# Differential attention scores: both components of a step issued together, in the order full, full, half, half, behind the first projections

## What is computed

```python
def diff_attention(q, k, v, pos, rel_bias, lam):
    scale = DIFF_HEAD_DIM ** -0.5
    def block(args):                        # 128 queries
        qb, qp = args
        s = jnp.einsum('bqhcd,bkhcd->bhcqk', qb, k).astype(jnp.float32) * scale
        bias = jnp.transpose(rel_bias[bucket], (0, 3, 1, 2)).astype(jnp.float32)
        s = s + bias[:, :, None]
        s = jnp.where(causal[:, None, None], s, NEG_INF)
        p = jax.nn.softmax(s, axis=-1)
        a = (p[:, :, 0] - lam * p[:, :, 1]).astype(v.dtype)
        return jnp.einsum('bhqk,bkhe->bqhe', a, v)
```

## Time and profile before

| | us |
|---|---|
| median of three runs | 2902.03 |
| the three runs | 2899.20 to 2904.88 |
| the profiled execution | 2900.93 |
| its span in the trace | 2899.5 |
| differential attention stage in it | about 397 to 655 |

### The profile page before, as it was taken

How to read it: one execution, slowest core, us unless ns; L and a number is a source line. 1 busy time by engine, 2 the same in 40 slices (tenths; PEclk the granted TensorE clock), 3 DMA queues, 4 the chain that set the end, 5 groups by cost and what they waited for, 6 DMA issues and landing times.

```text
span 2899.5 us, 46216 instructions
## 1 busy us (share of the span) xinstructions
PE 2749.4 (95%) x16516; PEld 2246.6 (77%) x16517; DVE 1502.7 (52%) x2607; ACT 1055.9 (36%) x1670; POOL 297.3 (10%) x318
## 2 busy tenths in 40 slices
PE   7899989988999997999999999999999999999995
PEld 3366655555666454989999999999899999999994
DVE  5555535664111145666666666665454445544454
ACT  2144324443110120545555555553333333333333
POOL 1000000000000123011111111111011111111111
PEclk9999989989999995999999999999999999999997
DMA  4000010002111434666666666667999999999995
GB/s 138 1 10 5 15 30 15 1 1 66 44 43 43 174 57 144 226 203 203 216 218 203 203 207 210 206 215 226 312 335 345 339 342 342 338 342 342 342 343 174
DMA packets 423534, 523.14 MB, mean 180 GB/s; under 512 B 27716, under 2 KB 334408, under 8 KB 423432
## 3 DMA queue, kind: packets, MB, share of 16 engines
q1 hardware_dynamic: 403544, 464.31, 49.4%
q0 software_dynamic: 18880, 57.91, 8.3%
q10 hardware_dynamic: 1040, 0.00, 0.0%
HBM read 482.23 MB, written 39.95 MB: 180 GB/s over the span
## 4 chain that ended last, share of the span: by engine, by line
PE 58%; issue 0%; DMA 0%; DVE 0%; ACT 0%; SPq 0%; POOLq 0%; POOL 0%; ACTq 0%
PE banks L2001 21%; PE banks L2011 19%; PE banks L2052 17%; PE banks L1993 1%; DMA arena<-acc_rows 0%; DVE arena L2295 0%; DMA acc_rows<-arena,rows 0%; ACT parts L2096 0%; SPq L1933 0%; DVE parts L2216 0%; ACT arena L2188 0%; ACT parts L2123 0%; ACT arena L2167 0%; POOLq L1959 0%; DVE stat L2293 0%
## 5 line engine op out<-in xcount | busy, mean ns | idle before, releaser
L2001 PEld LDWEIGHTS banks<-arena 128*128 128x128 f32 x5376 | 604.9, 192 | 8.3 <-issue 6.7
L2001 PE MATMUL banks<-arena 128*128 128x128 f32 x5376 | 605.2, 275 | 6.3 <-issue 6.3
L2011 PE MATMUL banks<-parts 128*128 128x256 f32 x4608 | 558.6, 284 | 7.1 <-issue 4.0
L2011 PEld LDWEIGHTS banks<-parts 128*128 128x128 f32 x4608 | 557.9, 193 | 8.7 <-issue 4.4
L2052 PE MATMUL banks<-parts 128*128 128x512 f32 x2160 | 498.3, 391 | 0.0
L2052 PEld LDWEIGHTS banks<-parts 128*128 128x128 f32 x2160 | 403.0, 188 | 82.1
L2212 DVE TENSOR_TENSOR parts<-arena,parts 128x1024 fp32r<-128x1024 f32 x264 | 315.2, 1222 | 128.4 <-ACT parts L2116 128.4
L2235 DVE TENSOR_SCALAR arena<-banks,arena 128x128 f32<-128x128 f32 (+1 forms) x528 | 181.3, 392 | 335.6 <-PE banks L2001 335.6
L2216 DVE TENSOR_TENSOR parts<-arena,parts 128x1024 fp32r<-128x1024 f32 x192 | 233.7, 1222 | 197.6 <-ACT parts L2123 196.6
L2116 ACT ACTIVATE parts<-arena 128x1024 fp32r<-128x1024 f32 x264 | 269.7, 1054 | 88.4 <-PE banks L2052 44.9
L2123 ACT ACTIVATE parts<-arena 128x1024 fp32r<-128x1024 f32 x192 | 201.1, 1054 | 178.3 <-PE banks L2011 123.4
(11 more groups left out here) (306 smaller groups left out, 2763.8 us busy)
## 6 DMA issues: line engine op xcount, KB each, us to landing
arena<-in_w SPq DMA_DIRECT2D x264, 1024.0 KB, 7.6
arena<-in_w SPq DMA_DIRECT2D x66, 2048.0 KB, 12.8
arena<-in_w_in SPq DMA_DIRECT2D x27, 512.0 KB, 5.4
arena<-in_x SPq DMA_DIRECT2D x16, 512.0 KB, 6.8
h_rows<-arena POOLq DMA_DIRECT2D x10, 512.0 KB, 7.6
acc_rows<-arena SPq DMA_DIRECT2D x8, 512.0 KB, 6.0
arena<-acc_rows SPq DMA_DIRECT2D x8, 512.0 KB, 7.4
out<-arena SPq DMA_DIRECT2D x8, 512.0 KB, 6.0
```

What stands on the lines that cost most here:

```text
L2001: last = nc.tensor.matmul(bank(g, 2 * (c % 2) + s)[:, a * JOB:a * JOB + P], w1[c][:, s, k, a * P:(a + 1) * P], xt[:, k, 0:P], start=(k == ...
L2011: last = nc.tensor.matmul(bank(g, 2 * (c % 2) + s)[:, a * JOB:(a + 1) * JOB], first_part[p][:, y, k, :], x[:, k, :], start=(k == 0 and y = ...
```

## The change

Both components of a step are now issued by one call, behind the first projections of the step. In every stretch of up to 512 keys the two full passes stand first, then the two half passes. The call waits for both exponentials of the step before, and for the projected units that component 1 needs. VectorE's and ScalarE's lists are the same as before.

```diff
-                def score(u, c):
+                def score(u):
                     h, i = divmod(u, TT)
-                    keys, s = (end(i) + 1) * P, 2 * u + c
-                    pe.wait_ge(lo_made, units_before(u, c, general))
-                    if s >= 2:
-                        pe.wait_ge(exped, s - 1)
-                    rows, cols = (first, second)[c], slice(i * P, (i + 1) * P)
+                    keys, cols = (end(i) + 1) * P, slice(i * P, (i + 1) * P)
+                    pe.wait_ge(lo_made, units_before(u, 1, general))
+                    if u >= 1:
+                        pe.wait_ge(exped, 2 * u)
                     for a in range(0, keys, HALF):
                         n = min(HALF, keys - a)
-                        out = bank(g, 2 * c + a // HALF)[:, 0:n]
-                        nc.tensor.matmul(out, q_c[c][:, cols], k_c[h % 2][c][:, a:a + n], start=True, stop=False)
-                        last = nc.tensor.matmul(out, q_c[c][rows, cols], k_low[h % 2][rows, a:a + n], start=False, stop=True)
-                    last.then_inc(scored, 1)
+                        outs = [bank(g, 2 * c + a // HALF)[:, 0:n] for c in range(2)]
+                        for c in range(2):
+                            nc.tensor.matmul(outs[c], q_c[c][:, cols], k_c[h % 2][c][:, a:a + n], start=True, stop=False)
+                        for c, rows in ((0, first), (1, second)):
+                            last = nc.tensor.matmul(outs[c], q_c[c][rows, cols], k_low[h % 2][rows, a:a + n], start=False, stop=True)
+                            if a + n == keys:
+                                last.then_inc(scored, 1)
...
-                score(0, 0)
-                score(0, 1)
+                score(0)
                 for u in range(DIFF_STEPS):
-                    if u + 1 < DIFF_STEPS:
-                        score(u + 1, 0)
                     for n, k in fill[u][0]:
                         project(n, k)
                     if u + 1 < DIFF_STEPS:
-                        score(u + 1, 1)
+                        score(u + 1)
                     for n, k in fill[u][1]:
                         project(n, k)
```

## The result

The changed kernel is **slower**: 2920.9 us (four runs, 2920.5 to 2923.3) against 2903.5 for the kernel before, a ratio of 1.0064 with a 95% interval of 1.0047 to 1.0082. That is +17.5 us in the medians, where +9 was forecast. The side was right, the size was half. The profiled execution has a span of 2919.9 us against 2899.5.

A forecast was written before the change was run, and what follows sets the result against it. The prediction took TensorE to limit the stage on the average. Order +3, clock +6 and last head's clock +2 gave +11, less 1 or 2 for slow stretches on waiting work: +9, 2911 us, range 2894 to 2922.

The forecast's parts named there:

- The saving: TensorE's score groups: two row-count changes in place of four, saving 6.5 or 4.6 us per head, 26 or 18 in all.
- the lower bound of the pair: Score half passes on disjoint rows run at the same time, so the second starts 0.02 us behind the first.
- the stream price of 0.22: Upper bound for score half passes: the second starts 0.22 us behind the first, as passes in a stream do.
- The waits: TensorE idles behind the chain of additions, maxima and exponentials: 6.6 us more per middle head, 6.3 with slower half passes.
- Before score i=6: a wait of **1.8: Middle head, ahead of tile 6's score: TensorE has 3.1 us of work against a chain of 4.7 + 0.15.
- The first head's -2: First head's change from the new order alone: -2 or -0.5 us, from a 0.79 wait gone and waits added.
- The +3 for the order as a whole: All heads, new order without clock effects: -0.4 or +6.2 us by half-pass overlap, with +3 taken between.
- the clock: TensorE falls to its lower clock behind half of some nine new idles, 1.4 us each: +6, and +2 in the last head.
- Same: Rival: clock stays up and half passes overlap, leaving the order alone, 0 to +5 us, 2902 to 2907; chance 0.34.
- Faster: Rival: waits ahead of tiles 4 and 6 under about 1 us each, so TensorE's saving shows: 2883 to 2896; chance 0.14.
- Slower still: Rival: pairing like passes hides no weight load, groups still cost 1.68 us, nothing pays for the waits: 2922; chance 0.07.
- Its sign: What would decide for the rival at 2922: the second full score pass starting 0.4 us behind the first.

The follow-up runs named there:

- extra passes: Changed kernel plus matrix passes with unread results, put into TensorE's idles where a bank is free: 2901.7 us, ratio 1.0001 to the kernel before.
- the scores first: Changed kernel with like passes still paired, but both components' scores ahead of the step's first projections: 2901.0 us, ratio 0.9994 to the kernel before.
- the last version above: Changed kernel with scores first, ScalarE's copies after both exponentials, subtraction after the combination, key unit earlier, extra passes in the last head: 2908.6 us, ratio 1.0020.

## Why the prediction was right in its side and wrong in its size

**The saving.** Forecast per middle head 6.5 or 4.6 us, by whether half passes overlap. They overlap: the lower bound of the pair holds, as the Trainium skill has it (TensorEngine Tiling, Key Properties: different tiles can load weights and multiply in parallel), with 0.50 us for the two here; the stream price of 0.22, taken from the rows, was too high. Measured is 5.9, the growth of the waits, 8.1, less that of the head, 2.2.

**The waits.** The chain of additions, maxima and exponentials was sized right at most places: 2.28, 1.01 and 2.48 us in place of 2.1, 1.0 and 2.8; in the first head 2.41 at unit 5's bank and 3.51 at unit 6's. In the last head the idle ahead of the third step is 3.16 for 3.7.

**A wait that was mis-sized.** "Before score i=6: a wait of **1.8**." The forecast let 1.71 us of projections run during that chain. In the middle heads they belong to the next key unit, in bank 7, and its first pass waits for the query unit's split, so they stand behind the wait and cover nothing. I had seen this in the first head and not looked for it in the others. The idle is 3.60. With it the waits of a middle head grew by 8.1 us (2.28, 3.60, 1.01 and 2.48, less the 1.23 before), not 6.6. For the order alone -0.2 was forecast for a middle head with overlapping halves, and 2.2 is measured at a clock of 1.00: 1.5 of the difference is waits, 0.6 the saving, and 0.3 a slip in the sum, since 58.5 + 6.6 - 6.5 is 58.6 and not 58.3. The first head's -2 does not follow from its terms either (1.1, 3.6 and 1.9 less 0.8 and 6.5 give -0.7); that the head grew by 1.7 with some 3.5 us more of missing clock (0.93 for 0.98), so by about -1.8 without it, bears out a figure that the working does not. The +3 for the order as a whole was thus near by errors that partly cancel, which is luck.

**The step that failed: the clock.** I gave it +6 in the stage and +2 in the last head, less 1 or 2, so 6 or 7 us, from half of nine idles at 1.4 each. The stage has 22 us more of missing clock than before. In the middle heads the clock alone is 6.6 and 4.9 us, 11.5 for the two, where I had put some 6 on the first three heads together, and in the stage extra passes took back 12.4. Three things were wrong. "If half bring the clock down": all nine idles were followed by a slow stretch, not half. "At 1.4 each": some stretches were longer than the one that I took the price from (6.8 us at 0.50 behind tile 4; eight passes in 5.37 and 6.57, for 5.08). And I took something off for slow time that falls on waits, where in the middle heads almost none did. The last head is 6.6 longer, where +2 for the order and +2 for the clock stood. With extra passes it took 57.4 us at 0.93, against 56.2 at 0.84 before, so most of its growth goes with the clock too, though there the two cannot be parted.

**The sum by these terms.** In the middle heads order, 2.2 twice, and clock, 6.6 and 4.9, are the 15.9 by which they grew (this is a division of the 15.9 by the one head measured at 1.00; that the clock part fits the missing clock, 6.7 and 5.2, is the check). With 1.7 and 6.6 in the outer ones it is 24.2, the stage's 24.4. In the profiled pair 4.0 of it did not show, since the changed kernel entered the stage earlier.

**The rivals.** "Same" needed a clock that stays up. The extra passes made that case in one middle head, which then cost 2.2 us; their run's 2901.7 looks like this rival's number, but owes 8.8 us to the expert stage and so does not confirm it. "Faster" needed waits under 1 us. "Slower still" named 2922, nearly the measured time, by a mechanism that is not there: a group costs 1.09 us, not 1.68. Its sign, though, was half met: the second full pass starts 0.34 behind the first, nearer to its 0.4 than to the forecast's 0.22. Its size is met by accident.

## What to carry to other kernels

Before a saving on the bound engine is added up, ask at each wait on the other engines what stood over it before, and read it again in every head or loop pass, not in the first alone. An order that makes the bound engine idle for two or three microseconds now and then pays a second time through its clock, in the middle heads here about half of each slow microsecond and more than twice the price of the order itself (11.5 against 4.4 us). Read the granted clock per window in both kernels before explaining a loss, and when an edit in one stage gains, check in the profiles that the gain lies in that stage: of the 19 us here only 12.4 did. Like passes, those on disjoint rows of the array above all, are worth placing side by side (17 us here), but ahead of the work that covers their consumers, not behind it.

## What the runs showed of the hardware

- Two fp32r passes of 512 columns, on rows 0 to 63 and on rows 64 to 127 and into different banks, took 0.50 us together, one alone 0.49.
- Going between 128-row and 64-row passes cost 0.42 us at 512 columns, in the expert stage's stream of 128-row passes 0.23. A pair of 128-row passes between 64-row ones was not a stream: the second started 0.34 us behind the first.
- Some 20 us of extra passes in idles (47 calls of 0.43 us) made the stage 12.4 us shorter and the kernel 19 us faster. The rest lies in the expert stage, where an idle of 6.46 us with no releaser in the profile was gone; the two runs with 47 calls lack it, the ten other profiles have one of 4.9 to 6.5 us. With 21 of the 47, at the head changes only, the kernel gained 1 us, as the clock fell elsewhere in the head.
- The granted clock was at its lower level, 1.2 GHz, behind all nine idles of 2.28 to 3.61 us in the changed kernel's first three heads, and behind one of 1.74 in the last version above. It stayed at its upper level in middle heads whose idles were under 1.3 us. It stayed up too behind an idle of 3.60 us in the first middle head of the run with extra passes, and behind 2.28 in head 1 with the scores first; the same idles one head later did bring it down. What decides between the two is left open.
